# Dense blocks of a two-block transformer forward pass: the first of three products as one pass of 512 columns, the other two as halves of 256

## What is computed

```
z = h @ w_in[l]                                             # 1024 x 4936
...
merged = gate_a * (y_a @ w_proj_a[l]) + gate_b * (y_b @ w_proj_b[l])
x = x + merged @ w_out[l]
h = rms_norm(x, norm_ffn[l])
u = causal_dwconv(h @ w_up[l], conv_w[l], conv_b[l])        # w_up 1024 x 5632
x = x + (jax.nn.silu(gat) * val) @ w_down[l]
...
h = h + mix @ w_out[layer]
h = h + (jax.nn.silu(hn @ w_gate[layer]) * (hn @ w_up[layer])) @ w_down[layer]
```

## Time and profile before

| | |
|---|---|
| median of 3 runs | 2344.11 us (2334.93, 2344.11, 2351.29) |
| the profiled execution | 2333.62 us, span of its trace 2331.8 us |
| granted TensorE clock, mean | 0.997 |
| TensorE, passes | busy 2293.4 us, 98% |
| TensorE, weight loads | busy 2119.8 us, 91% |
| VectorE / ScalarE / GpSimd | 46% / 27% / 67% |

### The profile page before, as it was taken

One profiled execution on the slowest core, in us unless ns is written; L12 is line 12 of the kernel. 1 busy time (PEld: TensorE's weight loads), 2 busy tenths in 40 slices (PEclk: granted clock), 3 DMA queues, 4 the chain that ended last, 5 costly groups with the idle time before them and its releaser, 6 DMA issues. The chain is left out here.

```text
span 2331.8 us, 50693 instructions
## 1 busy us (share of the span) xinstructions
PE 2293.4 (98%) x19134; PEld 2119.8 (91%) x19134; DVE 1068.9 (46%) x2156; ACT 618.7 (27%) x1355; POOL 1573.6 (67%) x818
## 2 busy tenths in 40 slices
PE   7999999999999999999999999999999999999997
PEld 6787699999999988876999999999998679999997
DVE  5776653364314436776534543143545854110112
ACT  4334710231101233347202311012322853000001
POOL 6564377777778775643677778777765447777775
PEclk9999999999999999999999999999999999999999
DMA  6223022223323322230223233322463002222232
GB/s 209 73 74 109 11 82 92 91 91 99 99 92 98 100 92 68 78 100 20 73 93 98 91 91 99 100 94 95 138 217 100 20 24 96 90 94 96 90 92 89
DMA packets 61631, 213.38 MB, mean 92 GB/s; under 512 B 6344, under 2 KB 6728, under 8 KB 61328
## 3 DMA queue, kind: packets, MB, share of 16 engines
q1 hardware_dynamic: 54368, 194.38, 26.2%
q10 hardware_dynamic: 7088, 16.58, 2.1%
HBM read 208.78 MB, written 10.01 MB: 94 GB/s over the span
## 5 line engine op out<-in xcount | busy, mean ns | idle before, releaser
L519 PE MATMUL out_tile<-arena_r,w_hi 128*128 128x256 f32 (+1 forms) x10352 | 1632.8, 280 | 0.0
L519 PEld LDWEIGHTS out_tile<-arena_r,w_hi 128*128 128x128 f32 x10352 | 1391.6, 189 | 0.5 <-issue 0.5
L519 PE MATMUL out_tile<-arena_r,w_lo 128*128 128x256 f32 (+1 forms) x5176 | 1040.9, 282 | 12.2 <-POOL w_lo L1960 7.5
L1954 POOL TENSOR_TENSOR w_hi<-weight_ring,cst 128x1024 fp32r<-128x1024 f32 (+1 forms) x348 | 656.7, 1887 | 520.8 <-PE out_tile L519 459.5
L1960 POOL TENSOR_TENSOR w_lo<-weight_ring,w_hi 128x1024 fp32r<-128x1024 f32 (+1 forms) x348 | 837.3, 2406 | 26.8
L519 PEld LDWEIGHTS out_tile<-arena_r,w_lo 128*128 128x128 f32 x5176 | 790.9, 189 | 40.7 <-issue 29.1
L1475 DVE TENSOR_TENSOR x<-out_tile,x 128x512 f32<-128x512 f32 x72 | 49.8, 692 | 354.6 <-PE out_tile L519 354.5
L1293 ACT ACTIVATE work<-out_tile,p 128x512 f32<-128x512 f32 x88 | 65.9, 774 | 395.3 <-PE out_tile L519 395.3
L1740 DVE SCALAR_TENSOR_TENSOR work<-out_tile,p,work 128x511 f32<-128x511 f32 x88 | 65.6, 745 | 211.8 <-ACT work L1293 211.8
L1979 POOL TENSOR_SCALAR work<-work,small 128x128 f32<-128x128 f32 (+2 forms) x60 | 34.9, 581 | 114.4 <-DVE small L1528 106.8
L1158 ACT ACTIVATE arena<-turned 128x128 f32<-128x128 f32 (+1 forms) x224 | 84.8, 430 | 47.2 <-PE turned L668 46.3
(11 more groups left out here) (223 smaller groups left out, 1923.4 us busy)
## 6 DMA issues: line engine op xcount, KB each, us to landing
weight_ring<-stream SPq DMA_DIRECT2D x356, 512.0 KB, 3.5
arena<-bias_rows ACTq DMA_DIRECT2D x4, 2048.0 KB, 10.8
bias_rows<-bias_kept ACTq DMA_DIRECT2D x2, 2556.0 KB, 22.6
bias_rows<-bias_kept SPq DMA_DIRECT2D x1, 2556.0 KB, 15.2
x<-x_t SPq DMA_DIRECT2D x4, 512.0 KB, 9.0
arena<-w ACTq DMA_DIRECT2D x1, 2048.0 KB, 10.2
out_t<-arena SPq DMA_DIRECT2D x8, 256.0 KB, 2.3
cst<-consts SPq DMA_DIRECT2D x1, 576.0 KB, 13.6
```

The costliest lines, as they stand in the source:

```text
L519: ins = pe.matmul(out[:, at], l, r[:, at], start=start and n == 0 and h == 0, stop=stop and n == 2, **kw)
L1954: pool.tensor_tensor(blocks_of(w_hi[:, s % SPLIT, :], used), blocks_of(ring[:, s, :], used), cols(cst, C_ONE).unsqueeze(1).to_broadcast([P ...
```

## The change

The first of the three products is no longer cut: one pass of all 512 columns. The other two remain halves of 256. Where `halves` has one member nothing changes.

```diff
                 for n, (l, r) in enumerate(((lhs[1], rhs[0]), (lhs[0], rhs[1]), (lhs[0], rhs[0]))):
-                    for h, at in enumerate(halves):
+                    for h, at in enumerate(halves if n else (slice(0, out.shape[-1]),)):
                         ins = pe.matmul(out[:, at], l, r[:, at], start=start and n == 0 and h == 0, stop=stop and n == 2, **kw)
```

## The result

The changed kernel is slower by 1.6%: a median of 2364.22 us in four runs against 2339.52 us of the kernel before in the same comparison, ratio 1.016 (95% interval 1.012 to 1.021); the ratio is taken over the fast runs alone, which leaves out 2351.29 us of before, and the medians of all runs differ by 1.1%. More striking than the median is the scatter. The changed kernel lies within 0.4 us (2363.98 to 2364.35); the kernel before, over all comparisons of this study, between 2303.24 and 2352.65 us. The forecast was 2354 us. The measured time lies inside both ranges given with it (2341 to 2367 us for the forecast's own case, 2321 to 2372 us over all cases); the ratio lies above the 1% within which the time was held to stay with 0.69.

The account below looks back on a forecast made before the run. TensorE's L519 passes, at 113.3 or 117.7 ns from start to start, were taken to bound the kernel. Wide passes add 9.9 + 0.4 = 10.3 us to the 2344.1 us median: 2354 us, range 2341 to 2367, over all cases 2321 to 2372.

Parts of the forecast that it names:

- the forecast's own case: Whole kernel: wide passes cost slightly more than two halves, 2354 us, with cost ends and scatter 2341 to 2367; chance 0.56.
- What bounds the kernel: TensorE passes at L519: matmul side busy 98%, never kept waiting for long, so the time between pass starts counts.
- The removed load costs nothing: L519, 2668 weight loads fewer: each is overlapped by the running pass, so removing them saves no time.
- GpSimd has cover: Weight split signalled 0.12 us later: about 0.94 of 1.06 us wait left, cost nothing; without cover 42 us.
- The price of a 512-column pass: L519: 232.8 to 235.7 ns from 384-column passes and L858, with 0.24 us in the trace as coarse check.
- the long blocks: L519 blocks at 117.7 ns a pass, 706.2 ns, some 1334 assumed; the change adds 0.3 ns each, 0.4 us.
- I take 234 ns beside the short pitch: L519 blocks at 113.3 ns a pass: one wide pass costs 234 ns where two halves cost 226.6 ns.
- the sum of 1334 x 7.4 ns: L519 blocks at 113.3 ns a pass: 1334 of them each grow by 7.4 ns, 9.9 us in all.
- a short block: L519 block at 113.3 ns a pass, 679.8 ns; some 1334 assumed, each predicted to grow by 7.4 ns.
- the sum of 10.3 us: Whole kernel: 9.9 us plus 0.4 us from L519 blocks at both pitches, added to the median of three runs, 2344.1 us.
- all at the long pitch: Rival, L519: a 512-column pass in each block throws every block onto 117.7 ns a pass, +36.0 us, 2370 us; chance 0.17.
- The scatter: Runs of before, 2334.9 to 2351.3 us: one or two long stretches at the other pitch; 500 blocks make 13.2 us.

Follow-up runs that it names:

- the streams: Sequences of float32r passes of chosen widths, appended after the last dense product of the kernel before, each from one TensorE stop to the next; their time says nothing.

## Why the prediction was wrong

*What bounds the kernel* held. L519 is TensorE's time, and every difference between the kernels here can be read from the pitch of its passes.

*The removed load costs nothing* held: the kernel with all products whole has 8028 loads fewer than before and is not faster. *GpSimd has cover* held, 7.4 us of waits, though the working was off: it took the 0.12 us by which the signal comes later off the wait (0.94 us left), and the wait grew to 1.29 us.

*The price of a 512-column pass* held in size. Extrapolated from 256 and 384 columns were 234.3 ns (and 232.8 ns by L858); in a stream of its own it takes 233.3 ns on average. For the long blocks I had 235.7 ns; it is 235.8. The formula for isolated passes of the Trainium skill (page "TensorE: Matmul & The Clock Gate", section "Back-to-back issue gap") gives an estimate of 215.8 ns and does not fit these float32r streams with a load for each pass; the rows of 384 columns had said so.

*The step that failed* is "I take 234 ns beside the short pitch", and with it the sum of 1334 x 7.4 ns: that the four other passes of a short block keep their 113.3 ns. They do not: with one 512-column pass in every block, none of the 2668 blocks is under 685 ns, where 1344 were before. A short block does not become 687.2 ns but 706.7 ns, +26.7 instead of +7.4. The long blocks are 706.7 ns before and after, +0 instead of +0.3. That half of the blocks are short, 1334, was an assumption and came out right (1344). Put with the right block, 1344 x 26.7 = 35.9 us. All blocks together take 1875.5 us before and 1907.2 us after, 31.7 us more; the other 4 us are in the blocks that hold a start or a stop of TensorE or come right behind one, which are cheaper after. Between the profiles are 30.6 us.

*Luck* brought 2354 us within 10 us of the measured 2364: the sum of 10.3 us stands on a base of 2344 us that was high. From the profiled execution it gave 2343.9 us, 20 us too low, for a time that was to grow by 30.6.

The rival "all at the long pitch" had the mechanism and, at 2370 us, nearly the time. The argument against it, that 256 and 384 columns both show short stretches, spoke of uniform streams, and the block is not one. The argument for it was one clause ("a rhythm the kernel has nowhere yet") and deserved more than 0.17: no row of the trace showed short passes beside a wide one, so the forecast stood on a case that was nowhere measured.

*The scatter* of before was read rightly as stretches at one or the other pitch. All of it: 2668 blocks at 26.7 ns are 71 us, from about 2293 us (all short, an estimate; no run showed it) to 2364 us (all long). The changed kernel sat at the upper end in every run. That also means that the ratio depends on how the runs of before fell: their medians in the comparisons here lay between 2321 and 2340 us, and my base of 2344 us from three runs was on the high side. Against 2344 us the change is 0.9%, against those medians 1.1 to 1.8%.

*Left open:* what inside the chip has the period of 768 columns, why 384 columns lead to the short pitch and 512 away from it, and why a start falls on one or the other. The granted clock is 1.00 at either pitch, and the streams show that no other engine and no transfer is needed; they name no part of the chip. All of them have a weight load for each pass and float32r operands: whether the loads or the type take part is not tested.

## What to carry to other kernels

When TensorE is full, look at the distance of starts before the durations, in windows without idle time, and in more than one execution: if equal passes show two distances and runs scatter by 2%, the time depends on how streams fall into step, and a change of shape can decide that for the whole kernel. Price a change of shape in the sequence in which it will stand; a wide pass was right on its own (233.3 ns) and cost 26.7 ns in company, in every block that had been short. Here a uniform stream of 256 columns was the best base, and 19 single passes of 384 columns ahead of its stretches, 3 us in all, took 18 us off the median.

## What was not expected of the hardware

- A uniform float32r stream (128 x 128 standing, a load for each pass, granted clock 1.00) has two steady pitches at 256 columns, 113.3 and 117.8 ns, and keeps either through some 3000 passes (second layer's feed-forward part: short in the first trace of before, long in the second).
- From the short one each further 128 columns take 60.0 ns in a uniform stream: 113.3, 173.3 and 233.3 ns, that is 0.469 ns a column less 6.7 ns. The 512-column stream is 231 and 236 ns in turn.
- The long one is 0.460 ns a column: 117.8 ns at 256, 235.8 ns for the wide pass in the changed kernel, 706.7 ns for 1536 columns as six of 256, with the first or the third product whole, and with the wide pass in every second block.
- One 512-column pass turned short streams long 30 times in 30, and so did every other single width tried but 384. One of 384 columns left every stream short, 14 in 14, four of which had been long; in the work it turned two of two.
- Single wide passes that come back after a multiple of 768 columns hold the stream at the long value (12 streams of 12, and three kernels); at other distances it goes as low as 0.450 ns a column. Two wide passes side by side in 1536 columns do not (0.4513 ns).
